# Dilated and full attention with values stationary: scaled probabilities stream, two heads in the halves of a bank

## What is computed

```python
def mixer_b(x, w_qkv, w_o, cos, sin):
    qkv = (x @ w_qkv).reshape(B, S, 3, 3, 16, 64)
    for g, (window, dil) in enumerate(((128, 1), (512, 4), (2048, 16))):
        q, k = apply_rope(qkv[:, :, g, 0], cos, sin), apply_rope(qkv[:, :, g, 1], cos, sin)
        o, lse = dilated_attention(q, k, qkv[:, :, g, 2], window, dil)   # softmax over the keys
    w = softmax(stack(lses), axis=0)        # together: one softmax over the keys of all three
    return sum(w * outs).reshape(B, S, 1024) @ w_o

x = layer_norm(ALPHA * x + mixer(x), ...)
x = layer_norm(ALPHA * x + swiglu(x, ...), ...)
```

## Time and profile before

| | us |
|---|---|
| median of 3 runs (2409.36 to 2410.32) | 2409.44 |
| span of the profiled execution | 2408.6 |
| TensorE busy in it | 2375.2 (99%) |
| VectorE busy | 1633.0 (68%) |
| ScalarE busy | 1122.9 (47%) |
| GpSimd busy | 184.1 (8%) |

### The profile page before, as it was taken

The page is one execution under the profiler, slowest core; times in us unless marked ns, Lnnn a source line. Parts: engine busy times, 40 slices in busy tenths (PEclk is TensorE's granted clock), DMA queues, the critical chain, the costliest instruction groups (busy, mean ns, idle before and its releaser), DMA issues.

```text
span 2408.6 us, 33578 instructions
## 1 busy us (share of the span) xinstructions
PE 2375.2 (99%) x13648; PEld 2001.8 (83%) x13648; DVE 1633.0 (68%) x2282; ACT 1122.9 (47%) x1570; POOL 184.1 (8%) x190
## 2 busy tenths in 40 slices
PE   7999999999999999999999999999999999999999
PEld 5788888787888878887888888888888888988887
DVE  7866755557667576668776777677676577687664
ACT  4544344444443434435443455564444365574442
POOL 1210002021000320001100100000000000001000
PEclk9999999999999999999999999999999999999999
DMA  6465343335553446543755344444755344445652
GB/s 247 142 202 209 140 175 140 141 140 171 197 209 140 163 165 215 191 158 128 262 188 179 136 175 157 155 179 149 279 180 188 113 167 156 173 175 181 225 177 91
DMA packets 259080, 419.09 MB, mean 174 GB/s; under 512 B 11984, under 2 KB 149200, under 8 KB 258928
## 3 DMA queue, kind: packets, MB, share of 16 engines
q1 hardware_dynamic: 254064, 400.15, 46.7%
q0 software_dynamic: 4864, 16.80, 2.1%
HBM read 415.86 MB, written 1.05 MB: 173 GB/s over the span
## 4 chain that ended last, share of the span: by engine, by line
PE 92%; DVE 4%; ACT 2%; DMA 1%; issue 1%; POOL 0%; SPq 0%; DVEq 0%; ACTq 0%
PE bank_L L2431 21%; PE bank_L L2447 17%; PE bank_S L2811 8%; PE bank_T L2776 7%; PE bank_L L2776 7%; PE bank_O L2811 7%; PE bank_L L2428 4%; PE bank_T L2781 4%; PE bank_L L2781 4%; PE bank_O L2724 1%; DVE wlo L1631 1%; PE bank_S L2431 1%; PE bank_O L2431 1%; PE bank_T L2398 1%; PE bank_T L2707 1%; PE bank_T L2386 1%
## 5 line engine op out<-in xcount | busy, mean ns | idle before, releaser
L1631 DVE TENSOR_TENSOR wlo<-raw,whi 128x2048 fp32r<-128x2048 f32 x316 | 718.0, 2290 | 123.4 <-ACT whi L1237 123.0
L1237 ACT ACTIVATE whi<-raw 128x2048 fp32r<-128x2048 f32 x290 | 542.5, 1894 | 55.3 <-DMA raw<-in_w_out 13.2
L2431 PE MATMUL bank_L<-whi,xt 128*128 128x512 f32 (+2 forms) x1632 | 495.8, 386 | 3.3 <-ACT tok L1283 2.1
L2447 PE MATMUL bank_L<-whi,xt 128*128 128x512 f32 x1248 | 389.2, 393 | 3.3 <-DVE xt L1645 2.1
L2431 PEld LDWEIGHTS bank_L<-whi,xt 128*128 128x128 f32 x1632 | 295.9, 188 | 61.2 <-ACT tok L1283 3.3
L2431 PE MATMUL bank_L<-wlo,xt 128*128 128x512 f32 (+2 forms) x816 | 311.4, 382 | 0.0
L2447 PEld LDWEIGHTS bank_L<-whi,xt 128*128 128x128 f32 x1248 | 230.6, 188 | 51.9 <-DVE arena L1737 2.9
L1503 ACT ACTIVATE tok<-tok 128x256 f32<-128x256 f32 x96 | 40.1, 417 | 449.5 <-DVE tok L2137 449.5
L2447 PE MATMUL bank_L<-wlo,xt 128*128 128x512 f32 x624 | 243.6, 390 | 0.0
L2776 PE MATMUL bank_T<-xt,whi 128*128 128x512 f32 x768 | 192.3, 392 | 0.0
L2776 PE MATMUL bank_L<-xt,whi 128*128 128x512 f32 x768 | 191.7, 392 | 0.0
(11 more groups left out here) (353 smaller groups left out, 3630.3 us busy)
## 6 DMA issues: line engine op xcount, KB each, us to landing
raw<-in_w_gate_up SPq DMA_DIRECT2D x176, 512.0 KB, 5.9
raw<-in_w_in SPq DMA_DIRECT2D x72, 1024.0 KB, 6.8
draw<-in_w_down SPq DMA_DIRECT2D x44, 1024.0 KB, 6.2
raw<-in_ffn_w_up SPq DMA_DIRECT2D x88, 512.0 KB, 5.8
raw<-in_b_w_qkv SPq DMA_DIRECT2D x36, 1024.0 KB, 6.9
draw<-in_ffn_w_down SPq DMA_DIRECT2D x22, 1024.0 KB, 6.2
raw<-in_w_lift SPq DMA_DIRECT2D x16, 1024.0 KB, 6.2
raw<-in_a_w_qkv SPq DMA_DIRECT2D x12, 1024.0 KB, 8.2
```

Source lines behind the costliest of these rows:

```text
L1237: act.activation(wide(whi, w, nkc, ncols)[:, ks, :], wide(raw, w, nkc, ncols)[:, ks, :], ACT.Copy) \
L1631: dve.tensor_tensor(wide(wlo, w, nkc, ncols)[:, ks, :], wide(raw, w, nkc, ncols)[:, ks, :], wide(whi, w, nkc, ncols)[:, ks, :].bitcast(F32 ...
L2431: mm = pe.matmul(banks[name][:, 0:st["ncols"]], xx[:, kk, t * P:(t + 1) * P], ww[:, kk, :], start=(kk == 0 and q == 0), stop=(kk == nkc - ...
L2447: mm = pe.matmul(banks[bank][:, :], xx[:, k, t * P:(t + 1) * P], ww[:, k, :], start=(k == 0 and q == 0), stop=(k == KC - 1 and q == 2))
```

## The change

The reciprocal now comes before the transposes: `pair_scales` multiplies the probabilities of pair i, in place, by the reciprocal of their sum, one instruction per head (B) or per head and half of the tokens (C). `pair_turned` waits for that (`scaled`) and no longer for the exponentials. The values become the stationary operand (64 columns) and 128 (in C 256 and 128) columns of transposed probabilities stream. Head w of the pair writes partitions 64 w to 64 w + 63. So the outputs have features on the partitions, and they stay in the bank: one bank collects 4 pairs in B (two groups per stage, now also in B0) and 2 pairs in C (four groups). From there ScalarE makes the high half (`group_high`) and VectorE the low one (`group_low`), without a transpose. Heads 0 to 7 go to `yt_hi` and `yt_lo`, heads 8 to 15 to `xt`; `Joined` lets the product with `w_o` read both. The scratch of the rope moves from `hg_values`, which lies on `yt_lo`, to `r`. Loads of gains and down weights wait for the counter of the values instead of that of the evacuations. The core of the diff:

```diff
-                    def pair_evacuate(j):
+                    def pair_scales(j):
                         act.wait_ge(rl_done, U0 + j + 1)
-                        act.wait_ge(pv_done, U0 + j + 1)
                         for w, u in enumerate(J[j]):
-                            for row, (_, _, o) in enumerate(u["rows"]):
-                                c = len(u["rows"]) * w + row
-                                ins = act.activation(o, banks[st["ob"][j % 2]][:, c * HD:(c + 1) * HD], ACT.Copy,
-                                                     scale=rl2[:, 4 * (j % 4) + c:4 * (j % 4) + c + 1])
-                        ins.then_inc(o_done, 1)
+                            for row in range(len(u["rows"])):
+                                mine = [q for q in u["pieces"] if q[0] == row]
+                                q = slice(u["ps"] + mine[0][1], u["ps"] + mine[-1][1] + mine[-1][2])
+                                c = 4 * (j % 4) + len(u["rows"]) * w + row
+                                ins = act.activation(smflat[:, q], smflat[:, q], ACT.Copy, scale=rl2[:, c:c + 1])
+                            ins.then_inc(scaled, 1)
+
+                    def group_high(g):
+                        to = st["to"]
+                        act.wait_ge(pv_done, U0 + (g + 1) * to["per"])
+                        act.activation(to["dst"][g][0], banks[st["ob"][g % 2]][:, :].rearrange("p (k s) -> p k s", s=SEQ),
+                                       ACT.Copy).then_inc(thi_done, 1)
...
                         if 1 <= i <= len(J):
                             pair_copies(i - 1)
-                        if i >= 2:
-                            pair_evacuate(i - 2)
+                        if i < len(J):
+                            pair_scales(i)
+                        if i >= 2 and (i - 1) % st["to"]["per"] == 0:
+                            group_high((i - 2) // st["to"]["per"])
                         if i in st["turns"]:
                             heads_hi(st["turns"][i])
-                        for g, _ in st["groups"].get(i, ()):
-                            group_hi(st["rows"], g)
...
+                    def group_low(g):
+                        to = st["to"]
+                        hi, lo = to["dst"][g]
+                        dve.wait_ge(thi_done, to["sg"] + g + 1)
+                        dve.tensor_tensor(lo, banks[st["ob"][g % 2]][:, :].rearrange("p (k s) -> p k s", s=SEQ), hi.bitcast(F32),
+                                          ALU.subtract).then_inc(tlo_done, 1)
...
                             pair_copies(i - 1)
-                            pair_reciprocal(i - 1)
+                        if i < len(J):
+                            pair_reciprocal(i)
+                        if i >= 2 and (i - 1) % st["to"]["per"] == 0:
+                            group_low((i - 2) // st["to"]["per"])
                         if i in st["ropes"]:
                             rotated(st["ropes"][i])
                         if i in st["splits"]:
                             split_lo(*st["splits"][i])
...
                     def pair_turned(j, w):
...
-                            pe.wait_ge(p_done, u["p0"] + 1)
+                            pe.wait_ge(scaled, u["sc0"] + 1)
...
                     def pair_values(j):
-                        name = st["ob"][j % 2]
-                        take(name)
-                        for w, u in enumerate(J[j]):
+                        to = st["to"]
+                        g, q = divmod(j, to["per"])
+                        name, o0 = st["ob"][g % 2], to["place"](q)
+                        if q == 0:
+                            take(name)
+                        for u in J[j]:
...
+                        for two in zip(*(u["pv"] for u in J[j])):
+                            for w, (c, width, v, o1, first, last) in enumerate(two):
+                                c += J[j][w]["pts"]
+                                mm = pe.matmul(banks[name][w * HD:(w + 1) * HD, o0 + o1:o0 + o1 + width], v, pflat[:, c:c + width],
+                                               start=first, stop=last)
                         mm.then_inc(pv_done, 1)
-                        held[name] = (o_done, U0 + j + 1)
+                        if q == to["per"] - 1:
+                            held[name] = (tlo_done, to["sg"] + g + 1)
...
                     if st["begun"]:
-                        turn_group(st["begun"]["rows"], 3)
                         output(st, 1, 1, 0, 4)
```

More of the change, by code:

```diff
@@ L76, in settle, with __init__, __getitem__ @@
         self.eng.wait_ge(self.sem, self.n - but)
+class Joined:
+    def __init__(self, first, rest, count):
+        self.first, self.rest, self.count = first, rest, count
+    def __getitem__(self, at):
+        p, k, c = at
+        return (self.first if k < self.count else self.rest)[p, k, c]
 def build(nc, x_in, positions, ln_g, ln_b, a_w_qkv, a_b_qkv, a_sinks, a_w_o, a_b_o, b_w_qkv, b_w_o, c_w_qkv, c_w_o,
@@ L456, in halves, with across, paired @@
             return st
-        def paired(pairs, first, qb, ob, ps_at, pts_at, fill=(), turns=(), ropes=(), splits=(), groups=(), parts=(), turned=None):
-            at_turns, at_groups = dict(turns), dict(groups)
+        def across(dst, per, place):
+            st = dict(dst=dst, per=per, place=place, sg=n["sg"])
+            n["sg"] += len(dst)
+            return st
+        def paired(pairs, first, qb, ob, ps_at, pts_at, to, fill=(), turns=(), ropes=(), splits=(), parts=()):
+            at_turns = dict(turns)
             st = add("paired", pairs=pairs, first=first, qb=qb, ob=ob, fill=[q for q, _, _ in fill], turns=at_turns,
-                     ropes=dict(ropes), splits=splits, groups=at_groups, parts=parts, rows=turned, out=None)
+                     ropes=dict(ropes), splits=splits, parts=parts, to=to, out=None)
             for late, a, b in fill:
@@ L480, in paired @@
                     u["edge"], u["banks"] = edge, bank + 1
+                    if len(u["rows"]) == T:
+                        v0, v1 = u["rows"][1][1]
+                        u["pv"] = [(0, T * P, v0, 0, True, False), (T * P, P, v1, P, False, True)]
+                    else:
+                        vs = u["rows"][0][1]
+                        u["pv"] = [(q * P, P, v, 0, q == 0, q == len(vs) - 1) for q, v in enumerate(vs)]
                     u["segs"] = [n["seg"] + 2 * q + w + 1 for q in range(bank + 1)]
@@ L621, in build @@
                 wo, bias, att = a_w_o[j], True, None
+                lhs = (tlo_done, [[hv["at"]["sg"] + k // 2 + 1 for k in range(KC)]] * T, (xt_hi, xt_lo))
             elif kind == 1:
@@ L651, in build @@
                         dst = vv[g] if which == 2 else next_tok()
-                        after = [(o_done, n["unit"])] if which == 2 and n["unit"] else []
+                        after = [(pv_done, n["unit"])] if which == 2 and n["unit"] else []
                         if (which, g) == (2, 2):
@@ L686, in build @@
                                   pts_at=lambda q, w: 768 * w if q % 2 else 384 * w)
+                    held_in = ((yt_hi, yt_lo), (xt_hi, xt_lo))[half]
+                    to.append(across([[q[:, 4 * half + 2 * g:4 * half + 2 * g + 2, :] for q in held_in] for g in range(2)],
+                                     4, lambda q: q * P))
                     if half == 0:
@@ L742, in build @@
                 part(late[0], 0, 3)
-                hv = halves(r)
+                both = across([[q[:, 2 * g:2 * g + 2, :] for q in (((yt_hi, yt_lo), (xt_hi, xt_lo))[g // 2])] for g in range(4)],
+                              2, lambda q: q * SEQ)
+                to = [both, dict(sg=both["sg"] + 2)]
                 pairs = []
@@ L758, in build @@
                 pool_splits([w1 + 1, w1 + 2, w1 + 3, w1 + 4, w1 + 5])
-                att = paired(pairs, first, SB, OB, lambda q, w: (2 * (q % 2) + w) * 384, lambda q, w: w * 384,
+                att = paired(pairs, first, SB, OB, lambda q, w: (2 * (q % 2) + w) * 384, lambda q, w: w * 384, both,
                              fill=[(late[0], 0, 1.4), (late[1], 1.4, 2.8), (late[2], 2.8, 5)], ropes=ropes_, turns=turns_,
@@ L2110, in _ @@
                             split_lo(*st["splits"][i])
-                        for g, _ in st["groups"].get(i, ()):
-                            group_lo(st["rows"], g)
                 elif st["kind"] == "ffn":
@@ L2662, in _ @@
                             output(st["out"], t, h, k0, k1)
-                        for g, _ in st["groups"].get(i, ()):
-                            turn_group(st["rows"], g)
                 elif st["kind"] == "attention":
```

60 lines of the change are left out of this document (21 added, 39 removed).

## The result

The changed kernel takes 2431.4 us (median of 4 runs, 2428.6 to 2433.7), the kernel before 2409.4 (4 runs, 2407.5 to 2410.3). The ratio is 1.0094, with a 95% interval from 1.0080 to 1.0108. The prediction was 2420 us with a range from 2406 to 2427, so the direction was right and the size was not: 22 us instead of 10.6.

A forecast was written before the change was run, and what follows sets the result against it. TensorE, busy 99% of the span, was taken as the bound. Net losses of 4.3 (B, first half), 2.2 (second) and 4.1 us (C) add 10.6 to 2408.6, plus 0.8 around it: 2420.0 us, range 2406 to 2427.

The forecast's parts named there:

- the rival that the two heads' streams run one after the other: In the values products of B and C, both heads' streams run in series: 2436 us, chance 5%.
- The gross gain of 8.6 us: TensorE in B and C: 1.6 us from cheaper values, 7 from dropped group transposes, their waits and queue change.
- The prices of the new work: Scales on ScalarE priced like exponentials of the same form: 1.78 us for a t = 1 pair, 1.5 for four in C.
- L0: Late evacuations of this bank: 1.0 and 1.2 us later in B's first half, 1.5 in turn 3 of its second.
- the rope behind B0: Behind B's first half, the second half's q rope stands behind the group's low half and ends 2.4 us late.
- O0: In B's second half, turn 5, values of pair 4 wait 3.7 us for group 0 to be copied out.
- the clock as a rival of 4%: At the O0 wait, the clock falls for one turn of 5 us, costing 5 more: 2425 us, chance 4%.
- VectorE's split: Turn 1 of B's second half: the reciprocal holds this weight split back, delaying maxima and bank copies: 0.45 us.
- turn 3: In C, the rope of k follows scales and group copies and makes TensorE 2.6 us later (2.1 to 3.2).
- the last turns of C: Turns 5 to 9, without filling products: copies, scales and splits in series delay the last output by 1.7 us.
- what lies around the span: Time outside the profiled span, 0.8 us (2409.44 - 2408.6), taken to stay the same.
- the likeliest case: Whole kernel: 2420 us, with the waits as worked out (2413 to 2427) given a chance of 68%.

The follow-up runs named there:

- all_six: all_four with three more orders: C's group copies early, rope ahead of the reciprocal, small logarithms moved behind C; 2401.9 us, ratio 0.9974 to the kernel before.
- wait_short: Kernel before, with the four products of the first rope behind B's first half made three times; profiled once, that stage cost 3.5 us more, no total given.
- outputs_first: Changed kernel, with the first part of the w_o product ahead of values and transposes in turns without filling products; 2430.1 us, ratio 1.0091.
- rope_first: Changed kernel, with the rope ahead of the group's low half on VectorE, behind B's first half and in C; 2423.6 us, ratio 1.0063.
- all_four: Changed kernel with rope ahead of low half, evacuations ahead of scales, group 0 copied early and outputs ahead of values; 2410.7 us, ratio 1.0011.
- evacs_first: Changed kernel, with evacuations of filling products ahead of the scales on ScalarE in two turns of each half of B; 2427.0 us, ratio 1.0075.
- scaled_before: Kernel before, with only reciprocal and scales moved ahead of the transposes; values, outputs and group transposes unchanged; 2425.6 us, ratio 1.0073.
- unscaled: Changed kernel without the scales of the probabilities, the group's copy multiplying by a constant 1/256 instead; 2416.6 us, ratio 1.0036.

## Why the prediction was too low

**TensorE's own work: right.** A values group of a pair with t = 0 takes 0.81 us to the next row, one with t = 1 1.46, predicted 0.80 and 1.44; before they were 0.85 and 1.55. TensorE's timeline of the changed kernel:

```profile
440.78 0.88 PE L2667 MATMUL bank_O<-pts,arena 128*64 128x128 f32 x12
441.59 0.88 PE L2646 MATMUL bank_T<-ident,sm 128*128 128x128 f32 x6
...
554.50 1.53 PE L2667 MATMUL bank_O<-pts,arena 128*64 128x128 f32 x24
555.96 0.87 PE L2646 MATMUL bank_T<-ident,sm 128*128 128x128 f32 x6
```

Half as many records, the same columns, nearly the same time: pricing by the columns that stream held, and the rival that the two heads' streams run one after the other falls. The gross gain of 8.6 us is borne out as far as 6.7, the sum of all_six's stages (5.9 with the shorter C).

**The prices of the new work: right.** Two scales of 768 columns take 1.76 us in one row, priced 1.78; four in C 1.50, priced 1.5. The waits that were named came out at their sizes: L0 at 1.7 and 1.9 us in B0 (predicted 1.7 and 1.9) and 1.5 later in B1 (1.5), the rope behind B0 2.75 (2.7), O0 3.4 (3.7). ScalarE's timeline in turn 5 of B1, then VectorE's, with the chain that O0 waited for:

```profile
558.11 1.76 ACT L1416 ACTIVATE sm<-sm,small 128x768 f32<-128x768 f32 x2 [0.23 <-DVE small L2124]
559.78 0.57 ACT L1422 ACTIVATE xt<-bank_O 128x512 fp32r<-128x512 f32 x1
```

```profile
560.38 0.69 DVE L2118 TENSOR_TENSOR xt<-bank_O,xt 128x512 fp32r<-128x512 f32 x1 [2.31 <-ACT xt L1422]
```

**The step that failed: the clock as a rival of 4%, for one place and one turn.** The prediction had four new waits of 1.7 to 3.7 us and held against a falling clock that the longest wait in these stretches, 1.0 us, had not brought it down. That row says nothing of waits two to four times as long. The clock should have been a term of the sum behind each of the long waits; the four falls cost 6.7 us, and with them the sum is 17.3. The Trainium skill (TensorE: Matmul & The Clock Gate, HAM oscillation), cited there, had it right that waits between bursts can bring the clock down; the runs agree, with falls behind waits of up to 4.9 us, wait_short's 2.2 among them, where nothing but the wait was added.

**Places that were missed,** 4.0 us together, all of the kind "who else stands behind this instruction". In turn 1 of B1 the prediction looked at VectorE's split; what waited longer was the values of pair 0, which need the arena (the projected values of the heads) from an evacuation that now stands behind the scales: 1.2 us instead of 0.45. In turn 2 of C the rope of q stands behind the reciprocal, which now waits for the exponentials, and two of its steps then take 1.1 us instead of 0.28, as the prediction had it only for turn 3: 1.0. In turn 3 TensorE lost 3.8 us instead of 2.6: the rope took 3.0 us where the prediction had 1.8, since its last two steps took 1.0 and 1.1 us beside casts on GpSimd. And behind B1 the last low half stands ahead of a split and the layer norm, which was in no sum: 1.1.

The two from the changed kernel's timelines, TensorE's in B1 and VectorE's in C:

```profile
534.36 0.88 PE L2667 MATMUL bank_O<-pts,arena 128*64 128x128 f32 x12 [1.16 <-ACT arena L1304]
```

```profile
842.12 1.13 DVE L1775 TENSOR_TENSOR r<-tok,rope_s 128x128 f32<-128x128 f32 x1
```

17.3 and 4.0 are 21.3, where the stages lost 20.4. The rest of the predicted chains (the last turns of C above all, 1.0 us instead of 1.7) came out 0.9 shorter than worked out.

The sum's last step has a small slip: it took 0.8 us for what lies around the span, the difference between a median and another execution's span. In every execution whose time and span are both on record it is 1.8 to 2.2 us.

**The range** ended where the waits of the likeliest case did. With the clock as a rival at one place it could not reach 2431.

**What stays open.** At about 2 us of wait the clock fell in some kernels and not in others: behind the same wait of 2.01 us for L0 it fell in the changed kernel and stayed full in outputs_first; behind that of the layer norm it fell in rope_first and stayed full in the changed kernel; in all_four it stayed full behind a wait of 2.14 us in C, in evacs_first it fell behind one of 1.6, in scaled_before behind one of 1.2. Behind the same 2.75 us behind B0 it fell in four kernels and stayed full in unscaled. In the three stages of all the profiles there are 31 waits of 2 us and more, and the clock fell behind 24 of them: behind all 11 from 3.1 us on, behind 13 of the 20 shorter ones. What decides below 3.1 us was not tried.

## What to carry to other kernels

A wait of TensorE that a change makes has two prices: its length, and often a half-speed stretch behind it, which cost 1.5 to 2.1 us each in the changed kernel and came behind 24 of the 31 waits of 2 us and more in all the profiles. Read the granted clock in windows of a microsecond or two around each wait, since the page's row is too coarse for it. When work moves from behind an engine's chain to ahead of it, list everything that stands behind it on the same engine, and write it behind what TensorE needs first: seven such orders turned the same change from 0.9% slower to 0.26% faster.

## What the runs showed that was not expected

A fall of the clock makes TensorE's busy time grow, so a kernel can look fuller and be slower: 2376.4 us busy at 0.996 of the clock against 2370.5 at 1.0 for the same instructions. And since the same wait can be followed by a fall in one execution and by none in another, a stage that an edit does not touch can cost more or less by some us: evacs_first gained 6.4 us in B and lost 3.0 in C, rope_first gained 8.9 in B0 and C and lost 2.1 in B1.
